# Gathering both matrices' rows of an expert with one request, in eight slots of 8 KB

## The reference

```
eid = take_along_axis(cid, ci)             # 128 expert numbers of a token
gate = softmax(cv).reshape(PEER_BLOCK, -1)
u = jnp.take(peer_u, eid, axis=0)          # one row of 1024 numbers per expert
vv = jnp.take(peer_v, eid, axis=0)         # another
a = gelu(einsum('td,ted->te', xb, u)) * gate
return einsum('te,ted->td', a, vv)
```

## Time and profile before

| | |
|---|---|
| median of 3 runs | 3712.04 us (3711.2 to 3724.84) |
| the profiled execution's own time | 3716.85 us |
| its span, first to last instruction | 3715.0 us |
| mean granted PE clock | 0.941 of full speed |

### The profile page before, as it was taken

The page is one execution under the profiler, slowest core; times in us unless marked ns, Lnnn a source line. Parts: engine busy times, 40 slices in busy tenths (PEclk is TensorE's granted clock), DMA queues, the critical chain, the costliest instruction groups (busy, mean ns, idle before and its releaser), DMA issues. The chain is left out here.

```text
span 3715.0 us, 47347 instructions
## 1 busy us (share of the span) xinstructions
PE 3230.7 (87%) x17102; PEld 2466.2 (66%) x17102; DVE 2509.4 (68%) x5666; ACT 1167.8 (31%) x2303; POOL 1893.7 (51%) x1500
## 2 busy tenths in 40 slices
PE   6999578999985988395999998999999999999898
PEld 5999467777874777385666666666666666666565
DVE  3001267776743799996777777777777777777776
ACT  3111223433423211195233322333333233333221
POOL 1000000000001244296888888888888888888885
PEclk8999779999987988698999999999999999999999
DMA  5232401111113100088999999999999999999997
GB/s 151 84 100 83 130 24 46 49 50 43 39 39 107 38 23 23 23 239 266 399 411 401 397 390 409 397 408 397 397 405 399 409 401 391 397 406 388 390 400 303
DMA packets 319313, 914.61 MB, mean 246 GB/s; under 512 B 30496, under 2 KB 128888, under 8 KB 301440
## 3 DMA queue, kind: packets, MB, share of 16 engines
q0 software_dynamic: 168144, 612.41, 42.0%
q1 hardware_dynamic: 150960, 299.49, 22.7%
HBM read 849.08 MB, written 63.93 MB: 246 GB/s over the span
## 5 line engine op out<-in xcount | busy, mean ns | idle before, releaser
L1199 DVE CUSTOM_DVE_ANT_0 ex_row_u<-ex_row_u,ex_h2n 128x1024 f32<-128x1024 f32 x576 | 710.0, 1233 | 263.6 <-DMA ex_row_u<-in_u_rows,eid 262.4
L1126 POOL DMA_INDIRECT ex_row_u<-in_u_rows,eid x570 | 760.0, 1333 | 164.1 <-issue 150.3
L1133 POOL DMA_INDIRECT ex_row_v<-in_v_rows,eid x576 | 739.6, 1284 | 194.3 <-issue 173.5
L1312 PE MATMUL ex_psum_v<-ex_a_hi,ex_v_hi 128*128 128x512 f32 x1024 | 432.8, 423 | 82.4 <-DVE ex_y L1245 77.9
L1296 PE MATMUL ex_psum_u<-h2d_hi,ex_u_hi 128*128 128x512 f32 x1024 | 408.7, 399 | 5.2 <-PEq L817 5.2
L1312 PE MATMUL ex_psum_v<-ex_a_hi,ex_v_lo 128*128 128x512 f32 x1024 | 405.7, 396 | 0.0
L1312 PE MATMUL ex_psum_v<-ex_a_lo,ex_v_hi 128*128 128x512 f32 x1024 | 404.3, 395 | 0.0
L1296 PE MATMUL ex_psum_u<-h2d_lo,ex_u_hi 128*128 128x512 f32 x1024 | 400.4, 391 | 0.0
L1296 PE MATMUL ex_psum_u<-h2d_hi,ex_u_lo 128*128 128x512 f32 x1024 | 400.0, 391 | 0.0
L1272 PE MATMUL ex_psum_g<-ex_row_v,ex_mask 128*32 128x512 f32 x2304 | 294.0, 630 | 102.6 <-DMA ex_row_v<-in_v_rows,eid 101.0
L390 POOL DMA_DIRECT2D rt_w_raw<-in_wq x2 | 1.1, 548 | 746.0 <-POOLq L1525 746.0
(11 more groups left out here) (319 smaller groups left out, 5992.0 us busy)
## 6 DMA issues: line engine op xcount, KB each, us to landing
ex_u_raw<-in_u SPq DMA_DIRECT2D x64, 1024.0 KB
ex_v_raw<-in_v SPq DMA_DIRECT2D x64, 1024.0 KB, 7.8
gates<-gt_out SPq DMA_DIRECT2D x8, 4096.0 KB, 16.6
ex_gate<-gates SPq DMA_DIRECT2D x64, 512.0 KB, 7.0
mx_pj<-proj SPq DMA_DIRECT2D x9, 1028.0 KB, 4.9
ex_row_u<-in_u_rows,eid POOLq DMA_INDIRECT x576, 8.3
ex_row_v<-in_v_rows,eid POOLq DMA_INDIRECT x576, 8.7
proj<-pj_out SPq DMA_DIRECT2D x36, 206.0 KB, 2.5
```

The lines of the kernel that those rows point to most:

```text
L1126: nc.gpsimd.indirect_dma_start(row_u[:, f % UR, :], None, u_rows, bass.IndirectOffsetOnAxis(eid[:, f:f + 1], 0)).then_inc(u_row[f % UR], 16)
L1133: nc.gpsimd.indirect_dma_start(row_v[:, f % VR, :], None, v_rows, bass.IndirectOffsetOnAxis(eid[:, f:f + 1], 0)).then_inc(v_row[f % VR], 16)
L1199: nc.vector.tensor_tensor_reduce(row_u[:, f % UR, :], row_u[:, f % UR, :], h2n[:, n % 2, :], 1.0, 0.0, ALU.mult, ALU.add, dots[:, k % DR, ...
L1312: last = nc.tensor.matmul(psum_v[:, i % VB, :], a[:, j, d * P:(d + 1) * P], b[:, (s - 1) % 2, j, :], start=(m == 0), stop=(m == 3 * JG - 1))
```

## The change

`peer_u` and `peer_v` are laid side by side in one array `uv_rows` of 8 KB rows, and one indirect DMA brings both rows of a token's 128 experts, 1 MB. There are eight slots of 8 KB in place of six and ten of 4 KB, three of them (`ex_rows`) in the part of memory that is there in `gate_matrices`, five (`ex_more_rows`) in `experts`; the sum stays 64 KB of a partition. A slot holds the u row and the v row of its token until the token's quad is done. 576 requests replace 1,152. The first three tokens' requests are issued early in place of six tokens' u requests. In the timetable the due time of dot f becomes (f - 3 + 5) / 9, and a quad is due as soon as its mask is.

```diff
-UR, VR = 6, 10
+ROWS, FIRST_ROWS = 8, 3
...
-    PER = 2 * GTOK // GROUPS
-    DUE = 10
+    PER = GTOK // GROUPS
+    DUE = 5
...
-                ready = self.put("dve", self.dots, (place["u", f] + self.DUE) / self.PER, f)
+                ready = self.put("dve", self.dots, (f - FIRST_ROWS + self.DUE) / self.PER, f)
             made = self.put("act", self.masks, ready + 0.03, k)
-            due = max(made + 0.05, now, (place["v", 4 * k + 3] + self.DUE) / self.PER)
+            due = max(made + 0.05, now)
...
-        row_v = sb("row_v", [P, VR, D])
+        more_rows = sb("more_rows", [P, ROWS - FIRST_ROWS, 2 * D])
...
-                for kind, f in table.fetches[UR:]:
-                    if kind == "u":
-                        pool.wait_ge(dotted, f - UR + 1)
-                        nc.gpsimd.indirect_dma_start(
-                            row_u[:, f % UR, :], None, u_rows,
-                            bass.IndirectOffsetOnAxis(eid[:, f:f + 1], 0)).then_inc(u_row[f % UR], 16)
-                    else:
-                        k = f // 4
-                        if f >= VR:
-                            pool.wait_ge(quad_done, (f - VR) // 4 + 1)
-                        nc.gpsimd.indirect_dma_start(
-                            row_v[:, f % VR, :], None, v_rows,
-                            bass.IndirectOffsetOnAxis(eid[:, f:f + 1], 0)).then_inc(v_row[f % VR], 16)
...
+                gate_mask(0)
+                for f in range(FIRST_ROWS, GTOK):
+                    if f >= ROWS:
+                        pool.wait_ge(quad_done, (f - ROWS) // 4 + 1)
+                    nc.gpsimd.indirect_dma_start(slot(f, 0, 2 * D), None, uv_rows,
+                                                 bass.IndirectOffsetOnAxis(eid[:, f:f + 1], 0)).then_inc(row[f % ROWS], 16)
+                    if f % 4 == 0:
+                        gate_mask(f // 4)
...
-                    dve.wait_ge(u_row[f % UR], 16 * (f // UR + 1))
+                    dve.wait_ge(row[f % ROWS], 16 * (f // ROWS + 1))
...
-                            pe.wait_ge(v_row[r % VR], 16 * (r // VR + 1))
+                            pe.wait_ge(row[r % ROWS], 16 * (r // ROWS + 1))
```

More of the change, by code:

```diff
@@ L811, in gathered, with gate_matrices @@
         self.gates_stored = [ctx.enter_context(nc.semaphore(f"ex_gates_stored{i}")) for i in range(2)]
-        self.u_row = [ctx.enter_context(nc.semaphore(f"ex_u_row{i}")) for i in range(UR)]
-def gate_matrices(nc, sel_i, sel_j, sel_g, iota, gates, u, ahead, u_rows, eid, h2_units, ident_d, eye_d):
+        self.row = [ctx.enter_context(nc.semaphore(f"ex_row{i}")) for i in range(ROWS)]
+def gate_matrices(nc, sel_i, sel_j, sel_g, iota, gates, u, ahead, uv_rows, eid, h2_units, ident_d, eye_d):
     with ExitStack() as ctx:
@@ L906, in _ @@
                 body(b, b == 0)
-                if b < UR:
+                if b < FIRST_ROWS:
                     nc.gpsimd.indirect_dma_start(
-                        ahead.row_u[:, b, :], None, u_rows,
-                        bass.IndirectOffsetOnAxis(eid[:, b:b + 1], 0)).then_inc(ahead.u_row[b], 16)
+                        ahead.rows[:, b, :], None, uv_rows,
+                        bass.IndirectOffsetOnAxis(eid[:, b:b + 1], 0)).then_inc(ahead.row[b], 16)
         @block.tensor
@@ L976, in __init__ @@
     def __init__(self):
[L977 to L982, removed]
         self.steps = STEPS + 3
@@ L1013, in put, with experts @@
         return t
-def experts(nc, hd, gates, u, v, u_rows, v_rows, x2, h2_units, y_rows, ahead, eid, gate_n):
+def experts(nc, hd, gates, u, v, uv_rows, x2, h2_units, y_rows, ahead, eid, gate_n):
     h_hi, h_lo = hd
@@ L1031, in experts @@
         u_raw, u_hi, u_lo = ahead.u_raw, ahead.u_hi, ahead.u_lo
-        ident, eye, row_u, h2n = ahead.ident, ahead.eye, ahead.row_u, ahead.h2n
+        ident, eye, h2n = ahead.ident, ahead.eye, ahead.h2n
         v_raw = sb("v_raw", [P, JG, D])
@@ L1056, in experts, with slot @@
         summed, added = sem("summed"), sem("added")
-        id_loaded, h2_loaded, u_row = ahead.id_loaded, ahead.h2_loaded, ahead.u_row
+        id_loaded, h2_loaded, row = ahead.id_loaded, ahead.h2_loaded, ahead.row
         xg_loaded, g_stored = ([sem(f"{n}{i}") for i in range(2)] for n in ("xg_loaded", "g_stored"))
-        v_row = [sem(f"v_row{i}") for i in range(VR)]
+        def slot(f, first, n):
+            i = f % ROWS
+            if i < FIRST_ROWS:
+                return ahead.rows[:, i, first:first + n]
+            return more_rows[:, i - FIRST_ROWS, first:first + n]
         dotted, g_active, gate_masked = sem("dotted"), sem("g_active"), sem("gate_masked")
@@ L1272, in gathered @@
                                 last = nc.tensor.matmul(psum_g[VQ * q:VQ * (q + 1), half, :], mask[:, k % MR, q, :],
-                                                        row_v[:, (4 * k + q) % VR, half * 512:(half + 1) * 512],
+                                                        slot(4 * k + q, D + half * 512, 512),
                                                         start=(m == 0), stop=(m == UQ - 1))
@@ L2247, in layer @@
             ahead.gathered(nc, ctx)
-            gate_matrices(nc, sel_i, sel_j, sel_g, iota, gates, I["u"], ahead, I["u_rows"], eid, h2_units, ident_d,
+            gate_matrices(nc, sel_i, sel_j, sel_g, iota, gates, I["u"], ahead, I["uv_rows"], eid, h2_units, ident_d,
                           I["consts"][:, C_EYE:C_EYE + VQ])
-        experts(nc, hd, gates, I["u"], I["v"], I["u_rows"], I["v_rows"], x2_tile, h2_units,
+        experts(nc, hd, gates, I["u"], I["v"], I["uv_rows"], x2_tile, h2_units,
                 rows(O["y_prompt"], O["y_sample"]), ahead, eid, gate_n)
```

22 lines of the change are left out of this document (11 added, 11 removed).

## The result

The changed kernel takes 3868.61 us (median of 3 runs, 3866.97 to 3877.36) against 3712.04: 1.0414 times as long, interval 1.0386 to 1.0441. The prediction was 3744 us in a range of 3665 to 3840. The sign was right, the size was not: 156.6 us are lost where 32 were forecast.

A forecast was written before the change was run, and what follows sets the result against it. The prediction took DMA to set the pace at 30.48 us a step. 3716.85 + 42 (slot loop) - 13 (start) + 3 (end) gave 3749 us on the profiled execution, 3744 us for the median, range 3665 to 3840.

The forecast's parts named there:

- the part on slots: Eight slots held until the quad is done: gather queue runs dry ahead of quad 63 only, then has a backlog.
- The table of "room": Per quad, parts of a step from its place to the first dot two quads later: -.02 to .42, least at 63.
- Loop: Slot round through quad 63: 124.6 us for four steps, 31.15 a step against 30.48, +42 us in all.
- Start: Before the loop: earlier requests and fewer dots ahead let step 1 begin near 1752, -13 us (0 to -16).
- End: Last two dots move into step 64 and the last quad comes later: +3 us (0 to +6).
- Fewer requests on POOL: 576 requests go from POOL, but nobody waits for POOL: gain nothing.
- The rate of 8 KB rows: Gathers go at 407 GB/s against 397, bounds 391 and 420; by this alone a step gains 0.6 us.
- The start from a dry queue: Start and end of a gather from a dry queue, beyond its bytes: 2.8 us (2.4 to 3.1).
- D: Rival: lateness at four quads adds to DMA's time, about half relieved: 32.4 us a step, 3823 us; chance 0.13.
- The sign that the prediction gave for D: In the new profile, steps near 33 us with DVE waits doubled.
- B: Rival: DMA stays the bound and 8 KB rows are cheaper, 29.2 to 30.4 us a step, 3620 to 3694; chance 0.20.
- C: Rival: slot loop and gain at the start cancel, 30.4 to 30.9 us a step, 3693 to 3731 us; chance 0.27.

The follow-up runs named there:

- experiment 13: Changed kernel with nine slots, room saved elsewhere with nothing left out, mask and quad places at every block, DUE 3: 3664.26 us, ratio 0.985 to the kernel before.
- 11: Changed kernel with ten slots, low part of h2 left out, mask and quad places at every block, DUE 3: 3634.55 us, ratio 0.9776 to the kernel before.
- experiments 7: Changed kernel, eight slots, with seven places for masks and ten for quads, one after each v block: 3713.76 us, ratio 1.0006 to the kernel before.
- experiment 8: Changed kernel, eight slots, seven mask and ten quad places, dots also due earlier (DUE 3 for 5): 3709.88 us, ratio 0.9989 to the kernel before.
- experiment 12: Changed kernel with separate 4 KB requests, u half refilled after its dot, places at every block, DUE 3: 3747.86 us, ratio 1.0084 to the kernel before.
- experiment 2: Changed kernel with ten slots for eight, the dense half leaving out the low part of h2: 3646.14 us, ratio 0.9823 to the kernel before.

## Why the prediction was wrong, step by step

**The step that failed** is in the part on slots: "So the queue runs dry ahead of quad 63, and after that has a backlog for the rest of the pattern." From it came the loop of 124.6 us for four steps, with eight batches of 13.3 us following one another without a hole. In the trace the queue runs dry at four places of nine quads, and those nine took 137.2 us. The other parts of that sum were near: the way from the last dot's start to the quad's start, 13.5 us, was 2810.5 - 2795.0 = 15.5, and the start 2.8 us (below). So the eight batches, with what lies between them, took 137.2 - 1.9 - 2.8 - 15.5 = 117.0 us instead of 106.4. These nine were slower than most: over the whole loop a pattern took 4 x 33.0 = 132 us. The table of "room" was right about which quad is tightest. But it asked only whether the first dot stood behind the quad that frees its slot; the first row needs 5.5 us and the fourth 14.5 us from the request, so a room of 0.06 or 0.17 of a step (2 to 5 us) is too little as well. And it took the places as times, though a dot that comes late pushes the work behind it to a later hour, and the next request with it. The first of the four holes is of this kind. By the places quad 64 stands 0.22 of a step, 7 us, behind quad 63; in the trace it came 14.2 us behind it. Quad 64 begins a group of eight, for which PE waits until DVE has copied the sums of the eight before (L1204), and that copy stands behind a dot that waited 4.96 us for its row:

```profile
2681.46 1.23 DVE L1194 CUSTOM_DVE_ANT_0 ex_more_rows<-ex_more_rows,ex_h2n 128x1024 f32<-128x1024 f32 x1 [4.96 <-DMA ex_more_rows<-in_uv_rows,eid]
...
2686.15 1.22 DVE L1204 COPY ex_quadrants<-ex_psum_g 128x1024 f32<-128x1024 f32 x1
```

```profile
2687.47 1.07 PE L1267 MATMUL ex_psum_g<-ex_rows,ex_mask 128*32 128x512 f32 x3 [6.54 <-issue]
```

**The terms.** Loop: +42 forecast, +159 measured; it is nearly the whole error, 117 us of 125. Start: -13 forecast, -13.1 measured; PE's first wait falls from 31.3 us to 21.19, not under 20. End: +3 forecast, +6.4 measured, just past its bound. Fewer requests on POOL: POOL is busy 581 us of 1600 where it was 1328, and nothing shows that it won time, as forecast; no run tests it by itself. The rate of 8 KB rows: 407 forecast and 407 measured; with the queue full it is 411 to 414 (506.91 MB / (0.771 x 1600) in experiment 13, 514.20 / (0.777 x 1600) in 11), inside the bounds of 391 to 420. The start from a dry queue: 2.8 us and the bytes of 1.05 MB at 420 GB/s, 2.5 us, make 5.3; measured 5.5. The Trainium skill's 2.0 us of fixed cost (page "DMA: Bandwidth & Descriptors", section "Anatomy of one DMA") would make it 4.5, an estimate with the same 2.5 us for the bytes; the trace is nearer to the 2.8.

**The rivals.** D was the right one, lateness that adds to DMA's time, and 0.13 was too little for it. It named four waits for a quad's first row: 3 us behind quad 60, 6 behind 61, 8 behind 63 and 3 behind 68. In the stretch above, where 69, 70 and 72 stand as 60, 61 and 63 do, they are 3.64, 5.46 and 6.25 us, and 2.12 behind 68:

```profile
2752.95 1.22 DVE L1194 CUSTOM_DVE_ANT_0 ex_rows<-ex_rows,ex_h2n 128x1024 f32<-128x1024 f32 x1 [2.12 <-DMA ex_rows<-in_uv_rows,eid]
...
2770.57 1.23 DVE L1194 CUSTOM_DVE_ANT_0 ex_more_rows<-ex_more_rows,ex_h2n 128x1024 f32<-128x1024 f32 x1 [3.64 <-DMA ex_more_rows<-in_uv_rows,eid]
...
2785.81 1.23 DVE L1194 CUSTOM_DVE_ANT_0 ex_rows<-ex_rows,ex_h2n 128x1024 f32<-128x1024 f32 x1 [5.46 <-DMA ex_rows<-in_uv_rows,eid]
```

The sign that the prediction gave for D nearly came true as well: 33.0 us a step, and DVE's waits 392 us where they were 215, 1.8 times. D's relief of half was too much: 33.0 us is 3.1 above DMA's 29.9, of the 5 us that it counted. What spoke against it, "while DVE waits the DMA engines work off their backlog", does not hold where the wait is for a queue that is empty. B's premise, cheaper 8 KB rows, was true and shows in experiments 11 and 13, where the queue stays full; with the eight slots and the timetable of the change it could not. C's number, no change, is where experiments 7 and 8 come out; that the same two terms cancel there was not tested. The rule of the Trainium skill, page "DMA: Bandwidth & Descriptors", section "Bandwidth", to batch transfers to 1 MiB or more, points to the gain of a full queue here (29.29 against 30.95 us a step in experiments 11 and 12, which differ in slots and in what they leave out too), and says nothing of the two lifetimes that the larger transfer ties together, which cost more in the changed kernel.

**What was not foreseen at all** is PE's clock. PE's work per step rose from 1466.40 / 1600 x 30.48 = 27.9 us to 1398.57 / 1600 x 33.0 = 28.8, with the same instructions. How that comes about is below. It is a consequence, as experiment 2 shows; how much of the 2.5 us a step is due to it stays open, as no run held the clock while the queue ran dry.

## What to carry to other kernels

Joining two transfers joins their lifetimes: the half that is used first is then held as long as the half that is used last, and the request for the next waits for the later of the two. Before joining, compare the round of a slot (from the request to the landing of the last of its batch, to the last use, to the next request, with every wait for a place in an order) with slots times pace, at the tightest place of the order. Here that is 31.9 us against 27.1; it shows that room is missing, not how much time that costs. Places nearer to the use brought the loss of 4.1% back to nothing (experiment 8), and one slot more on top of them made it a gain of 1.5% (experiment 13). A wait on the issuing engine says little by itself: look whether the queue behind it has run dry.

## What the runs showed of the hardware

**TensorE came back at half its clock after a short stop.** In the stretch above PE waits 6.24 us for DVE; its next matmuls begin 0.42 us apart, and some 5 us later 0.23 us apart:

```profile
2794.41 0.79 PE L1307 MATMUL ex_psum_v<-ex_a_hi,ex_v_hi 128*128 128x512 f32 x1 [6.24 <-DVE ex_y L1240]
2795.01 0.63 PE L1307 MATMUL ex_psum_v<-ex_a_lo,ex_v_hi 128*128 128x512 f32 x1
2795.43 0.63 PE L1307 MATMUL ex_psum_v<-ex_a_hi,ex_v_lo 128*128 128x512 f32 x1
...
2799.68 0.40 PE L1307 MATMUL ex_psum_v<-ex_a_lo,ex_v_hi 128*128 128x512 f32 x1
2799.91 0.40 PE L1307 MATMUL ex_psum_v<-ex_a_hi,ex_v_lo 128*128 128x512 f32 x1
```

```profile
2794.00:2797.00 3.00, 2.59 (x6) 1.82 (x6) 2.95 (x6) 0.00 (x0) 0.00 (x0) 0.50 1.03 433
2799.70:2804.00 4.30, 4.30 (x20) 3.55 (x19) 3.86 (x6) 0.00 (x0) 0.00 (x0) 1.00 1.01 423
```

The granted clock is 0.50 (1.2 GHz) in the first window and 1.00 (2.4 GHz) in the second. The kernel before, whose waits of PE for rows and for DVE are at most 4.1 us long in its window, was granted 0.99 over it. So here a stop cost PE the wait and then some 5 us of slow matmuls behind it.

**8 KB rows went faster than 4 KB rows from a full gather queue:** 411 to 414 GB/s (experiments 11 and 13) against 394 to 397 (experiment 12 and before), 4 to 5%.
